# The modulation rows of a two-layer diffusion backbone: eight products spread over four column tiles of the TensorE array

## What is computed

```python
silu_c = jax.nn.silu(c)
silu_cc = jax.nn.silu(c_ctx)
for l in range(DEPTH):
    sh1, sc1, g1, sh2, sc2, g2 = jnp.split((silu_c @ w_mod[l] + b_mod[l])[:, None, :], 6, axis=-1)
    csh1, csc1, cg1, csh2, csc2, cg2 = jnp.split(silu_cc @ w_mod[l] + b_mod[l], 6, axis=-1)
    h = rmsnorm(x, norm1_g[l]) * (1.0 + sc1) + sh1
...
```

## Time and profile before

| | us |
|---|---|
| median of 3 runs | 3909.63 (3906.82 to 3919.57) |
| profiled execution: its own time | 3925.83 |
| profiled execution: span | 3924.0 |
| PE busy in the span | 3748.6 (96%) |
| DVE busy | 2791.2 (71%) |
| ACT busy | 2027.1 (52%) |
| mean granted clock of PE | 0.983 of full |

### The profile page before, as it was taken

One profiled execution on the slowest core, in us unless ns is written; L12 is line 12 of the kernel. 1 busy time (PEld: TensorE's weight loads), 2 busy tenths in 40 slices (PEclk: granted clock), 3 DMA queues, 4 the chain that ended last, 5 costly groups with the idle time before them and its releaser, 6 DMA issues.

```text
span 3924.0 us, 60588 instructions
## 1 busy us (share of the span) xinstructions
PE 3748.6 (96%) x22454; PEld 3164.9 (81%) x22454; DVE 2791.2 (71%) x5634; ACT 2027.1 (52%) x4198; POOL 0.2 (0%) x4
## 2 busy tenths in 40 slices
PE   8999999999999999999999999989899999969998
PEld 4775687788886899999996788868588888857887
DVE  3546743499969688888668766665765899697666
ACT  3344432466667555555556544444354666674443
POOL 0000000000000000000000000000000000000000
PEclk9999999999999999999999999999998999999999
DMA  5212222356544455555553455533034555504554
GB/s 185 84 65 76 102 89 99 102 180 185 182 155 140 134 183 186 182 184 184 183 184 119 143 187 184 185 113 112 7 123 138 173 189 184 186 8 144 185 185 160
DMA packets 142196, 568.30 MB, mean 145 GB/s; under 512 B 15808, under 2 KB 17344, under 8 KB 130240
## 3 DMA queue, kind: packets, MB, share of 16 engines
q1 hardware_dynamic: 142016, 566.14, 44.7%
HBM read 565.03 MB, written 1.05 MB: 144 GB/s over the span
## 4 chain that ended last, share of the span: by engine, by line
PE 84%; DVE 13%; ACT 1%; issue 1%; DMA 0%; SPq 0%; DVEq 0%; ACTq 0%
PE ps L529 55%; PE ps L945 12%; PE ps L963 9%; PE ps L947 6%; DVE arena L1624 6%; DVE low L1624 3%; ACT arena L1114 1%; PE ps L737 1%; DVE ring_low L1624 1%; DVE arena L2116 0%; DVE arena L2107 0%; DVE arena L2109 0%; DVE XT L2197 0%; DVE arena L2113 0%; DMA ring<-wmod_in 0%
## 5 line engine op out<-in xcount | busy, mean ns | idle before, releaser
L1114 ACT ACTIVATE high<-ring 128x512 fp32r<-128x512 f32 x1632 | 1028.6, 632 | 1037.3 <-PE ps L529 502.9
L1624 DVE TENSOR_TENSOR low<-ring,high 128x512 fp32r<-128x512 f32 x1632 | 1075.8, 688 | 290.8 <-ACT high L1114 279.4
L529 PE MATMUL ps<-h_pair,high 128*128 128x512 f32 x3456 | 1240.1, 401 | 17.1 <-DVE h_pair L1624 10.1
L529 PE MATMUL ps<-h_pair,low 128*128 128x256 f32 x3456 | 971.9, 281 | 0.0
L529 PEld LDWEIGHTS ps<-h_pair,high 128*128 128x128 f32 x3456 | 653.3, 189 | 177.9 <-issue 11.9
L945 PE MATMUL ps<-wt,high 128*128 128x512 f32 x2048 | 725.3, 399 | 5.7 <-DVE low L1624 5.7
L529 PEld LDWEIGHTS ps<-h_pair,low 128*128 128x128 f32 x3456 | 657.2, 190 | 0.0
L947 PE MATMUL ps<-wt,low 128*128 128x256 f32 x2048 | 575.8, 281 | 0.0
L1114 ACT ACTIVATE arena<-ps 128x256 f32<-128x256 f32 (+3 forms) x658 | 274.3, 426 | 437.5 <-PE ps L529 406.8
L529 PE MATMUL ps<-arena 128*128 128x128 f32 (+8 forms) x2456 | 399.1, 318 | 85.9 <-ACT arena L1114 70.2
L945 PEld LDWEIGHTS ps<-wt,high 128*128 128x128 f32 x2048 | 385.5, 188 | 102.4 <-issue 3.0
(11 more groups left out here) (174 smaller groups left out, 4227.3 us busy)
## 6 DMA issues: line engine op xcount, KB each, us to landing
ring<-u_in SPq DMA_DIRECT2D x384, 512.0 KB, 3.5
ring<-v_in SPq DMA_DIRECT2D x384, 512.0 KB, 3.5
ring<-win_in SPq DMA_DIRECT2D x56, 1024.0 KB, 4.9
ring<-wmod_in SPq DMA_DIRECT2D x24, 1024.0 KB, 5.0
ring<-wq_in SPq DMA_DIRECT2D x48, 512.0 KB, 3.6
ring<-wmod_in SPq DMA_DIRECT2D x48, 512.0 KB, 3.7
ring<-wbr_in SPq DMA_DIRECT2D x16, 768.0 KB, 4.3
ring<-wout_in SPq DMA_DIRECT2D x8, 1024.0 KB, 4.9
```

What stands on the lines that cost most here:

```text
L529: return pe.matmul(o, l_, r, start=first, stop=last)
L1114: return act.activation(o, i_, f, **kw_)
L1624: return dve.tensor_tensor(o, a, b, op)
```

## The change

A row's eight products now go to the four 32-column tiles of the array in turn. Product k has a stationary operand 32 columns wide (`csil[:, 2k:2k+32]`: block k's two columns and 30 that belong to the next blocks or are padding), and writes 32 partitions of the bank, from partition 32 (k mod 4). Each tile accumulates two of the eight products. In the bank, partitions 0, 32, 64 and 96 hold four partial sums of the first vector, and the partitions behind them four of the second; the other partitions hold sums that nobody wants. ACT copies all 128 partitions x 256. The turn is now a full fp32 product: the copied row (128 x 128) is stationary and a table `V_SUM` of 128 x 2 with a one at p mod 32 = 0 or 1 streams, so that it turns and adds the four partial sums, and drops the rest. `csil` and `vec` get a few columns more, and PE waits once for `vec` at the start. The order of the instructions on every engine stays as it was.

```diff
         sp.dma_start(vec[:, :, :], vec_in).then_inc(*inc("vec_in", by=16))
-            sp.dma_start(csil[:, :, :], c_in).then_inc(*inc("c_in", by=16))
+            sp.dma_start(csil[:, :], c_in).then_inc(*inc("c_in", by=16))
...
+            def mod_part(b, k, w):
+
+                p = 32 * (k % 4)
+                return mm(b[p:p + 32, 0:256], csil[:, 2 * k:2 * k + 32], w, k < 4, k >= 4)
+
             def mod_row(l, n):
...
                 for k in range(KB):
-                    i = mm(b[0:2, 0:256], csil[:, k, :], w[:, k, :], k == 0, k == KB - 1)
+                    i = mod_part(b, k, w[:, k, :])
                 i.then_inc(*inc("mod_row", l, n))
...
                 for j in range(2):
                     c = 2 * (2 * n + j)
-                    i = pe.transpose(to[:, c:c + 2], rows[0:2, n % 2, j * P:(j + 1) * P], ident[0:2, 0:2])
+                    i = mm(to[:, c:c + 2], rows[:, n % 2, j * P:(j + 1) * P], vec[:, 0, V_SUM:V_SUM + 2])
...
             pe.wait_ge(*at("kept_in"))
+            pe.wait_ge(*at("vec_in"))
...
                         kk = 4 * (m % 2) + k
-                        i = mm(ps[row % 2][0:2, 0:256], csil[:, kk, :], w[:, k, :], kk == 0, kk == KB - 1)
+                        i = mod_part(ps[row % 2], kk, w[:, k, :])
...
-            fn(csil[:, :, :], csil[:, :, :], ACT.Silu).then_inc(*inc("csil"))
+            fn(csil[:, :], csil[:, :], ACT.Silu).then_inc(*inc("csil"))
...
-                fn(rows[0:2, n % 2, :], b[0:2, 0:256], ACT.Copy).then_inc(*inc("mod_row_read", l, n))
+                fn(rows[:, n % 2, :], b[:, 0:256], ACT.Copy).then_inc(*inc("mod_row_read", l, n))
...
+            (np.arange(P)[:, None] % 32 == np.arange(2)[None, :]).astype(np.float32)], axis=1))
```

More of the change, by code:

```diff
@@ L57 @@
 C_KEPT, C_ALL = 384, 1664
-V_N1, V_N2, V_BMOD, V_CW, V_CB, V_SSDN, V_MLN, V_QN, V_KN, V_BIAS, V_ALOG, V_D = (
-    0, 8, 16, 64, 94, 100, 104, 108, 109, 110, 142, 158)
-V_ALL = 166
+V_N1, V_N2, V_BMOD, V_CW, V_CB, V_SSDN, V_MLN, V_QN, V_KN, V_BIAS, V_ALOG, V_D, V_SUM = (
+    0, 8, 16, 64, 94, 100, 104, 108, 109, 110, 142, 158, 166)
+V_ALL = 168
+C_COLS = 2 * KB + 30
 def shape_constants():
@@ L140, in write_program @@
         vec = sb("vec", [P, DEPTH, V_ALL])
-        csil = sb("csil", [P, KB, 2])
+        csil = sb("csil", [P, C_COLS])
         mod = sb("mod", [P, DEPTH, 48, 2])
@@ L2309, in lay_out @@
     x = x.reshape(T, KB, P).transpose(2, 1, 0)
-    c = np.stack([columns(f["c_ctx"]), columns(f["c"][0])], axis=2)
+    c = np.stack([columns(f["c_ctx"]), columns(f["c"][0])], axis=2).reshape(P, 2 * KB)
+    c = np.concatenate([c, np.zeros((P, C_COLS - 2 * KB), np.float32)], axis=1)
     w = f["w_in"]
@@ L2340, in lay_out @@
             columns(np.tile(f["att_qnorm"][l], 2)), columns(np.tile(f["att_knorm"][l], 2)),
-            np.broadcast_to(rows, (P, rows.size))], axis=1))
+            np.broadcast_to(rows, (P, rows.size)),
+            (np.arange(P)[:, None] % 32 == np.arange(2)[None, :]).astype(np.float32)], axis=1))
     vec = np.stack(vec, axis=1)
```

## The result

The changed kernel takes 3869.5 us, the median of 4 runs (3863.9 to 3873.9), against 3911.1 us before (4 runs): a ratio of 0.9882, 95% interval 0.9867 to 0.9898. That is about 46 us less by the ratio, where 58 were forecast, and 18 us above the forecast of 3851, inside the range. A second timing of both gave 0.9884 (0.9864 to 0.9904). The kernel before took 3911 us in one session and 3919 in the others, so I compare ratios, and stages within traces.

The account below looks back on a forecast made before the run. PE was taken to bound the head and layer 0's scan, and the gate products only through the rows. Gains of 13.5 (head), 29 (scan) and 16 (gate products) sum to 58.5 us, giving 3851 us, range 3836 to 3874.

Parts of the forecast that it names:

- A row's cost: Modulation rows on PE: four tiles at once make a row 1.0 us; row and turn fall from 3.76 to 1.45 us.
- partial packing: Rival for all rows: no more than two tiles run together, a row takes 1.87 us, total 3863 us; chance 0.13.
- the tiles take turns: Rival for all rows: column tiles do not overlap, a row takes 4.4 us, total 3957 us, slower; chance 0.08.
- The head: Before `modulation`: the wait for PE's turn goes and DVE's chain is what is late next; gain 13.5 us, ends 11 and 15.
- up to 2 us: In the head: the cost allowed in case the sums of squares begin at half clock.
- The gate products: Layer 0's two passes fall to DVE's pace, as in layer 1: gains 5.4 and 10.7, together 16 us, ends 11 and 17.5.
- 30.4 groups' worth: In the gate products: layer 1's pass of 103.4 us divided into DVE's own pace of 3.40 us a group.
- The scan: Layer 0's scan falls from 141 to 112 us, PE at 93%; gain 29 us, ends 6 and 37.
- the scan gives little back: Rival: granted clock falls or the DVE-PE chain is tighter; layer 0's scan gains 10 us, total 3870; chance 0.13.
- The likeliest case: Whole kernel: the forecast of 3851 us with its own range of 3837 to 3866; chance 0.63.

Follow-up runs that it names:

- e_move: Changed kernel with the second row and its turn in each step of layer 0's scan moved ahead of the products awaiting masked decays; ratio 0.9893 to the kernel before.

## Why the prediction was right, and where it was wrong

**A row's cost: right.** 1.00 us from row to turn, forecast 1.0, from a pair of 64-column products. Four tiles run at once, and the row is as short as four steps at the full pace of 0.216 us make it. So "partial packing" and "the tiles take turns" are both out. The rule of the Trainium skill's "TensorE: Matmul & The Clock Gate" (its part on packing small matmuls) that a load overlaps with running matmuls only across row groups is not borne out here: all 16 loads use the same 128 rows, each takes 106 to 110 ns, 1.7 us end to end, and the row as a whole takes 1.00 us. The turn was undersized: 0.53 us for 0.45. Four steps of 0.118 us are 0.47 already, and the sum had no passage to the next shape (0.09 us for the row).

**The head: right in its mechanism, with an end that was too narrow.** Forecast 13.5 us, 11 to 15; 13.8 in the first traces. The second traces have `modulation` at 52.6 and 41.9, a gain of 10.8 us. In that trace of the changed kernel row 2 and its turn ran at half clock, so that the sums of squares start 1.6 us later than above, and they ran partly at half clock themselves, which costs 2.3 us. Timeline, beside the 7.11 us above:

```profile
20.81 9.39 PE L530 MATMUL ps<-arena,kept 128*128 128x512 f32 x16
```

The "up to 2 us" that I allowed for this was too little (3.8 us), and it comes in most traces: of the eight other kernels with packed rows in the head, five start `modulation` at 41.0 to 42.1, and three at 37.9 to 38.9.

**The gate products: right.** 5.9 + 10.7 = 16.6 us, forecast 5.4 + 10.7 = 16. The stage without rows in layer 1 was a ready measurement of what the stage would become. A side figure was wrong without effect: between the first and last of 32 multiplications lie 31 steps of 3.34 us, not "30.4 groups' worth" of 3.40.

**The scan: the step that failed.** "DVE at 89% makes 109 us of the whole scan, PE at 93% makes 112. I take 112, a gain of 29 us." It gave back 4 to 6 us. The sum took both shares from a step of layer 1 at full clock. What happened is the rival "the scan gives little back", at a chance of 0.13, by the first of its two reasons, the granted clock. I had argued against it that PE would still be over 90% busy. In fact PE is 89% busy by its records (126.6 of 142.0), half clock included, and 83% in the stretch at full clock, where DVE is at 95%. What is shown: more work on PE, of either kind, brings the clock back and shortens the scan by 8 to 18 us, while the same work in another order (`e_move`) leaves both about as they are (0.85, 139.1 us). The kernel with both scans filled reached 123.9 us with 10 us of dead work in it, a gain of 22 us over before where 29 were forecast. So most of the forecast gain was there, and the clock withheld it. What exactly lowers the clock in this stage stays open; four gaps of 1.6 to 2.3 us, with the added work beside them, did not.

**The sum.** By stages of the second traces of both: head 10.8, scan 6.1, gate products 16.6, the stretch between the passes 4.9, the rest -2.1, together 36.3 us of span. The first traces give 13.8, 4.1, 16.6, 5.8 and a rest of 11.6, together 51.9, with 6.7 of the rest in the stretch that varies by itself. The timed runs say 42 to 46, between the two.

**What was luck.** The time came inside the range only because the rival's 3870 had been taken into it. The likeliest case by itself ended at 3866 and missed. That 3870 and 3869.5 agree so closely is luck too: the rival gave the scan 10 us, it brought 4 to 6, and some 5 us came from the stretch between the passes, which no part of the prediction had.

## What to carry to other kernels

When a change takes work from an engine that was always busy, ask what its clock does once it is not: PE lost some 36 us of work in a stage and the stage became only 4 to 6 us shorter, because it ran at half clock for about a third of its time. A stage of the same kernel that lacks the work in question shows beforehand what the stage without it may become, its clock too: layer 1's scan had stood at a clock of 0.86 and 0.82 in the two traces of before. Products of one sum with few columns can go to the four column tiles, here in two orders alike, with a turn that also adds: 1.53 us for row and turn instead of 3.76.

## What the runs showed of the hardware that was not expected

- Unread products made the kernel faster: 10 us of them in the scan took 11 to 13 us off it, at a granted clock of 0.99 instead of 0.82 and 0.84.
- Two products in the same column tile, one behind the other in the list, did not hold up the next tile's: a row took 1.02 us so, and 1.00 us with neighbours in different tiles.
- A shift of the arena by 34 numbers for each partition went with 0.5% less time over 800 us of products whose program was the same (800.3 to 796.5 us, 1415 records in 200 us for 1405).
